# A hybrid encoder step on one Trainium2 core: running maximum in attention, scaling on ScalarE, side work moved from GpSimd to VectorE

## The reference, cut to what matters

```
h = x + 0.5 * post1(SwiGLU_1(pre1(x)))          # F1
u = pre_mix(h); z = u @ w_in                     # IP: q|k|v, rwkv r,k,v,lora, gates
A = differential attention(z)                    # 4 heads, two softmax maps each
B = RWKV-7 time mixing(z)                        # 8 heads of 64
h = h + post_mix((sigmoid(gA)*(A@w_o_att) + sigmoid(gB)*(B@w_o_rwkv)) @ w_out)   # OP
y = h + 0.5 * post2(SwiGLU_2(pre2(h)))           # F2

attention of one head:  a = softmax(s0) - lam * softmax(s1);  o = a @ v
                        o = o * rsqrt(mean(o*o) + EPS) * subln_g * (1 - lam_init)
token mix of RWKV:      zs = z + (prev - z) * mu         # r, k, v and the lora columns
output of RWKV:         out = (norm(y) * lnx_g + lnx_b + bonus) * g
```

## Time and profile before

| | |
|---|---|
| median of 3 runs | 3108.46 us (3101.37 to 3112.38) |
| the profiled execution's own time | 3106.88 us |
| its span, first to last instruction | 3105.1 us |
| PE busy | 3005.9 us (97%) |
| DVE busy | 1768.8 us (57%) |
| ACT busy | 1301.8 us (42%) |
| POOL busy | 593.9 us (19%) |
| mean granted TensorE clock | 0.988 |

### The profile page before, as it was taken

How to read it: one execution, slowest core, us unless ns; L and a number is a source line. 1 busy time by engine, 2 the same in 40 slices (tenths; PEclk the granted TensorE clock), 3 DMA queues, 4 the chain that set the end, 5 groups by cost and what they waited for, 6 DMA issues and landing times.

```text
span 3105.1 us, 59030 instructions
## 1 busy us (share of the span) xinstructions
PE 3005.9 (97%) x23912; PEld 2663.9 (86%) x23912; DVE 1768.8 (57%) x3001; ACT 1301.8 (42%) x2682; POOL 593.9 (19%) x850
## 2 busy tenths in 40 slices
PE   8999999999999999999989999999999999999997
PEld 8999989888888878899778798888787889899997
DVE  5456543644674463665666545757756846656444
ACT  4434444432434443533444444444534434444432
POOL 1001002312621421501501302303213201010000
PEclk9999999999999999999999999999999999999999
DMA  6445557644654664643644644526455424665443
GB/s 170 126 129 174 155 175 221 205 151 133 215 189 151 217 194 142 212 125 96 227 154 148 211 148 131 169 76 222 141 166 162 129 89 138 207 207 169 127 127 120
DMA packets 504493, 500.51 MB, mean 161 GB/s; under 512 B 29096, under 2 KB 402112, under 8 KB 504208
## 3 DMA queue, kind: packets, MB, share of 16 engines
q1 hardware_dynamic: 475968, 406.36, 42.1%
q0 software_dynamic: 28256, 90.39, 9.3%
HBM read 443.16 MB, written 54.47 MB: 160 GB/s over the span
## 4 chain that ended last, share of the span: by engine, by line
PE 88%; DVE 6%; issue 2%; ACT 2%; POOL 1%; DMA 1%; SPq 0%; ACTq 0%; POOLq 0%; DVEq 0%
PE ps L279 42%; PE ps L289 29%; PE ps L1065 5%; DVE wlo L243 1%; PE ps L1846 1%; PE ps L1830 1%; PE ps L301 1%; PE ps L1764 1%; PE ps L1057 1%; PE ps L1775 1%; PE ps L1801 1%; PE ps L1840 1%; PE ps L1070 1%; PE ps L1197 1%; ACT whi L235 1%
## 5 line engine op out<-in xcount | busy, mean ns | idle before, releaser
L243 DVE TENSOR_TENSOR wlo<-raw,whi 128x512 fp32r<-128x512 f32 x1140 | 823.1, 724 | 830.0 <-ACT whi L235 827.3
L235 ACT ACTIVATE whi<-raw 128x512 fp32r<-128x512 f32 x1140 | 712.6, 628 | 629.0 <-PE ps L279 348.3
L279 PE MATMUL ps<-xnhi,whi 128*128 128x384 f32 x2688 | 929.6, 346 | 3.4 <-DVE xnlo L556 3.4
L279 PE MATMUL ps<-xnhi,wlo 128*128 128x384 f32 x2688 | 903.2, 336 | 0.0
L279 PE MATMUL ps<-xnlo,whi 128*128 128x384 f32 x2688 | 902.4, 336 | 0.0
L279 PEld LDWEIGHTS ps<-xnhi,whi 128*128 128x128 f32 x2688 | 507.7, 189 | 28.9 <-issue 14.5
L279 PEld LDWEIGHTS ps<-xnlo,whi 128*128 128x128 f32 x2688 | 508.0, 189 | 2.7 <-issue 2.2
L279 PEld LDWEIGHTS ps<-xnhi,wlo 128*128 128x128 f32 x2688 | 507.0, 189 | 0.0
L289 PE MATMUL ps<-whi,hidhi 128*128 128x512 f32 x936 | 383.5, 410 | 13.8 <-DVE xnlo L556 9.7
L289 PE MATMUL ps<-whi,hidlo 128*128 128x512 f32 x936 | 367.9, 393 | 0.0
L289 PE MATMUL ps<-wlo,hidhi 128*128 128x512 f32 x936 | 367.6, 393 | 0.0
(11 more groups left out here) (310 smaller groups left out, 3411.8 us busy)
## 6 DMA issues: line engine op xcount, KB each, us to landing
raw<-in_ffn_w_in_dram SPq DMA_DIRECT2D x528, 256.0 KB, 3.0
raw<-in_ffn_w_out_dram SPq DMA_DIRECT2D x264, 256.0 KB, 2.9
raw<-in_w_in_dram SPq DMA_DIRECT2D x252, 256.0 KB, 3.0
xt<-h_scratch SPq DMA_DIRECT2D x42, 512.0 KB, 5.9
att<-in_cache_att_k_dram POOLq DMA_DIRECT2D x64, 256.0 KB, 4.8
att<-in_cache_att_v_dram POOLq DMA_DIRECT2D x64, 256.0 KB, 3.1
rw<-zr_scratch POOLq DMA_DIRECT2D x51, 256.0 KB, 7.5
raw<-in_w_out_dram SPq DMA_DIRECT2D x48, 256.0 KB, 3.1
```

The source lines that it names most:

```text
L235: act.activation(B["whi"][:, slot], B["raw"][:, slot], ACT.Copy).then_inc(E["whi"], 1)
L243: dve.tensor_tensor(B["wlo"][:, slot], B["raw"][:, slot], B["whi"][:, slot].bitcast(F32), ALU.subtract).then_inc(E["wlo"], 1)
L279: ins = pe.matmul(ps[:, bank, 0:BT], B["w" + wt][:, n % RING, i * P:(i + 1) * P], x(xt, i), start=first and i == 0 and (wt, xt) == passes[ ...
```

## The change

Six edits, which the diff shows. (1) In attention with two chunks the second chunk's maximum is taken together with the first's (a running maximum), so only the first chunk has to be rescaled later: one ACT exponential of two columns, one ACT pass over map 0's first 512 columns (`att_sc`). The softmax's common factor 1/sum of map 0 is left out of the weights; it comes back in the norm after V (as ACT's `scale` in the square and one more small product on POOL). The pass L2040 and one small operation go; the chunks are turned last first. (2) From the second stage on, x is scaled on ACT instead of DVE, and a pre norm has 9 steps. (3) The last post norm multiplies the gain in ahead of the mean square, in halves, and makes scale and residual one pass. (4) The token mixes of the recurrence move from POOL to DVE, one to two steps later or earlier; POOL keeps the loads; its waits for them and for the slots of the mixes go to DVE with the work (lines that only move are left out of the diff). (5) So do the four output operations of `C3` and `C4`. (6) `timetable()` counts a slot as 0.6 in the first 17 slots of OP and in slots 2 to 7 of a stage that follows on a whole stage with a post norm, so fewer side steps fall there; `O` costs 1.5.

```
-POST_STEPS, PRE_STEPS, POST_LEAD = 15, 8, 6
+POST_STEPS, PRE_STEPS, POST_LEAD = 15, 9, 6
...
+            for tl in range(NT):
+                if k:
+                    act.wait_ge(E["rstd"], 3 * (posts + pres) + tl + 1)
+                    act.wait_ge(E["squared"], squares)
+                    act.activation(B["xt"][:, tl], B["xt"][:, tl], ACT.Identity, scale=sums[:, 4 + tl:5 + tl]).then_inc(E["x2d"], 1)
+                yield
-            for _ in range(PRE_STEPS - 5):
+            for _ in range(PRE_STEPS - 8):
...
-            for _ in range(4):
-                yield
-                dve.wait_ge(E["rstd"], 3 * (posts + pres) + tl + 1)
-                dve.tensor_scalar(B["xt"][:, tl], B["xt"][:, tl], rstd[:, tl:tl + 1], None, ALU.mult).then_inc(E["x2d"], 1)
+                if k == 0:
+                    dve.wait_ge(E["rstd"], 3 * (posts + pres) + tl + 1)
+                    dve.tensor_scalar(B["xt"][:, tl], B["xt"][:, tl], rstd[:, tl:tl + 1], None, ALU.mult).then_inc(E["x2d"], 1)
-            for _ in range(PRE_STEPS - 7):
+            for _ in range(PRE_STEPS - 3):
...
-        for _ in range(POST_LEAD + 2):
+        def gained(tl, hf):
+            y = B["yb"][:, tl, hf * 512:(hf + 1) * 512]
+            dve.wait_ge(E["gain_in"], 16 * (posts + 1))
+            dve.wait_ge(E["squared"], 6 * (posts + pres) + 3 * hf + tl + 1)
+            dve.tensor_tensor(y, y, B["gB"][:, hf * 512:(hf + 1) * 512], ALU.mult).then_inc(E["scaled"], 1)
+        for step in range(POST_LEAD + 2):
+            if last and step >= POST_LEAD - 1:
+                gained(step - POST_LEAD + 1, 0)
+        if last:
+            for tl in range(NT):
+                gained(tl, 1)
+            for tl in range(NT):
+                dve.wait_ge(E["rstd"], 3 * (posts + pres) + tl + 1)
+                dve.wait_ge(E["xin%d" % tl], 16 * (posts + pres + 1))
+                dve.wait_ge(E["scaled"], 3 * posts + 4 + tl)
+                dve.scalar_tensor_tensor(B["yb"][:, tl], B["yb"][:, tl], rstd[:, tl:tl + 1], B["xt"][:, tl], ALU.mult, ALU.add).then_inc(E["h_done"], 1)
-                if step < NT:
-                    scale(step)
-                    add(step)
+                pass
...
+        lora = slot(S_L)
+        dve.wait_ge(E["rw_ld_l"], 48 * (p + 1))
+        own.do(dve.tensor_tensor(lora[:, 256:512], lora[:, 256:512], lora[:, 0:256], ALU.subtract))
+        own.do(dve.tensor_tensor(lora[:, 256:512], lora[:, 256:512], slot(S_ML)[:, 0:256], ALU.mult))
+        dve.tensor_tensor(lora[:, 0:256], lora[:, 0:256], lora[:, 256:512], ALU.add).then_inc(E["rw_zl"], 1)
+        dve.wait_ge(E["rw_ld_r"], 48 * (p + 1))
+        own.do(dve.tensor_tensor(slot(S_RP), slot(S_RP), slot(S_R), ALU.subtract))
+        own.do(dve.tensor_tensor(slot(S_RP), slot(S_RP), slot(S_MU), ALU.mult))
+        dve.tensor_tensor(slot(S_R), slot(S_R), slot(S_RP), ALU.add).then_inc(E["rw_mix"], 1)
+        dve.wait_ge(E["rw_ld_k"], 48 * (p + 1))
+        own.do(dve.tensor_tensor(slot(S_KP), slot(S_KP), slot(S_K), ALU.subtract))
+        own.do(dve.tensor_tensor(slot(S_KP), slot(S_KP), slot(S_MK), ALU.mult))
+        dve.tensor_tensor(slot(S_K), slot(S_K), slot(S_KP), ALU.add).then_inc(E["rw_mix"], 1)
+        dve.wait_ge(E["rw_ld_v"], 32 * (p + 1))
+        dve.wait_ge(E["rw_ld_mv"], 16 * (p + 1))
+        own.do(dve.tensor_tensor(slot(S_VP), slot(S_VP), slot(S_V), ALU.subtract))
+        own.do(dve.tensor_tensor(slot(S_VP), slot(S_VP), slot(S_MU), ALU.mult))
+        dve.tensor_tensor(slot(S_V), slot(S_V), slot(S_VP), ALU.add).then_inc(E["rw_mix"], 1)
...
+        dve.wait_ge(E["rw_ln"], 32 * (p + 1))
+        dve.wait_ge(*done(E, "yn", p + 1))
+        own.do(dve.tensor_tensor(y, y, slot(Z_LG if kd else S_LG), ALU.mult))
+        own.do(dve.tensor_tensor(y, y, slot(Z_LB if kd else S_LB), ALU.add))
+        own.do(dve.tensor_tensor(y, y, slot(S_BON), ALU.add))
+        dve.wait_ge(*done(E, "gg", p + 1))
+        dve.tensor_tensor(y, y, slot(S_GG), ALU.mult).then_inc(E["rw_out"], 1)
...
-        mix(l2[:, S_L, 0:256], l2[:, S_L, 256:512], l2[:, S_ML, 0:256]).then_inc(E["rw_zl"], 1)
-        mix(slot(S_R), slot(S_RP), slot(S_MU)).then_inc(E["rw_mix"], 1)
-        mix(slot(S_K), slot(S_KP), slot(S_MK)).then_inc(E["rw_mix"], 1)
-        mix(slot(S_V), slot(S_VP), slot(S_MU)).then_inc(E["rw_mix"], 1)
+        yield "G"
-        yield "G"
...
-            act.activation(st[:, 8:12], st[:, 8:12], ACT.Exp).then_inc(E["att_f"], 1)
+            act.activation(st[:, 8:10], st[:, 8:10], ACT.Exp).then_inc(E["att_f"], 1)
+            act.wait_ge(E["att_f"], two_before(n) + 1)
+            act.wait_ge(E["att_ex"], 2 * chunks_before(n + 1))
+            act.activation(V["ex"][0][:, 0:512], V["ex"][0][:, 0:512], ACT.Identity, scale=st[:, 8:9]).then_inc(E["att_sc"], 1)
-        for c, (a, e) in enumerate(chunks_of(tile)):
-            act.wait_ge(E["att_t"], chunks_before(n) + c + 1)
-            act.activation(V["awT"][:, a // P:e // P], ps[:, AB[c], 0:e - a].rearrange("p (k q) -> p k q", q=P), ACT.Copy).then_inc(E["att_tev"], 1)
+        for i, c in enumerate(turned(nc)):
+            a, e = chunks_of(tile)[c]
+            act.wait_ge(E["att_t"], chunks_before(n) + i + 1)
+            act.activation(V["awT"][:, a // P:e // P], ps[:, AB[i], 0:e - a].rearrange("p (k q) -> p k q", q=P), ACT.Copy).then_inc(E["att_tev"], 1)
...
-        act.activation(V["oh"][:, tile - TILE0[blk]], ps[:, AB[0], 0:P], ACT.Square, accum_out=st[:, 20:21]).then_inc(E["att_sq"], 1)
+        act.activation(V["oh"][:, tile - TILE0[blk]], ps[:, AB[0], 0:P], ACT.Square, scale=st[:, 12:13], accum_out=st[:, 20:21]).then_inc(E["att_sq"], 1)
...
-            dve.tensor_scalar(nb, nb, SCALE, None, ALU.mult).then_inc(E["att_nb"], 1)
-            if c == 1:
+            if c == 0:
+                dve.tensor_scalar(nb, nb, SCALE, None, ALU.mult).then_inc(E["att_nb"], 1)
+            else:
+                dve.scalar_tensor_tensor(nb, nb, SCALE, st[:, 0:2], ALU.mult, ALU.min).then_inc(E["att_nb"], 1)
-                own.do(dve.tensor_tensor(st[:, 12:14], st[:, 0:2], st[:, 2:4], ALU.min))
-                pair = lambda x: x.rearrange("p (c m) -> p c m", c=2)
-                dve.tensor_tensor(pair(st[:, 8:12]), st[:, 12:14].unsqueeze(1).broadcast_to([P, 2, 2]), pair(st[:, 0:4]), ALU.subtract).then_inc(E["att_df"], 1)
+                dve.tensor_tensor(st[:, 8:10], nb, st[:, 0:2], ALU.subtract).then_inc(E["att_df"], 1)
-        if nc == 1:
-            own.do(dve.reciprocal(st[:, 12:14], st[:, 4:6]))
-            own.do(dve.tensor_tensor(st[:, 16:18], st[:, 12:14], lamv, ALU.mult))
-        else:
+        total = st[:, 4:6] if nc == 1 else st[:, 14:16]
+        if nc == 2:
-            own.do(dve.tensor_tensor(st[:, 4:8], st[:, 4:8], st[:, 8:12], ALU.mult))
-            own.do(dve.tensor_tensor(st[:, 12:14], st[:, 4:6], st[:, 6:8], ALU.add))
-            own.do(dve.reciprocal(st[:, 12:14], st[:, 12:14]))
-            own.do(dve.tensor_tensor(st[:, 12:14], st[:, 12:14], lamv, ALU.mult))
-            own.do(dve.tensor_tensor(pair(st[:, 16:20]), pair(st[:, 8:12]), st[:, 12:14].unsqueeze(1).broadcast_to([P, 2, 2]), ALU.mult))
-        for d, (a, e) in enumerate(chunks_of(tile)):
+            own.do(dve.tensor_tensor(st[:, 4:6], st[:, 4:6], st[:, 8:10], ALU.mult))
+            own.do(dve.tensor_tensor(total, st[:, 4:6], st[:, 6:8], ALU.add))
+        own.do(dve.reciprocal(st[:, 12:14], total))
+        own.do(dve.scalar_tensor_tensor(st[:, 16:17], total[:, 0:1], neg_lam, st[:, 13:14], ALU.mult, ALU.mult))
+        for c in turned(nc):
+            a, e = chunks_of(tile)[c]
-            own.do(dve.tensor_scalar(x0, x0, st[:, 16 + 2 * d:17 + 2 * d], None, ALU.mult))
-            dve.scalar_tensor_tensor(x0, x1, st[:, 17 + 2 * d:18 + 2 * d], x0, ALU.mult, ALU.add).then_inc(E["att_aw"], 1)
+            ratio = st[:, 16:17]
+            if nc == 2 and c == 0:
+                ratio = st[:, 17:18]
+                own.do(dve.tensor_tensor(ratio, st[:, 16:17], st[:, 9:10], ALU.mult))
+                dve.wait_ge(E["att_sc"], two_before(n) + 1)
+            dve.scalar_tensor_tensor(x0, x1, ratio, x0, ALU.mult, ALU.add).then_inc(E["att_aw"], 1)
...
-        pool.tensor_tensor(st[:, 22:23], st[:, 22:23], halfc, ALU.pow).then_inc(E["att_rs"], 1)
+        pool.tensor_tensor(st[:, 22:23], st[:, 22:23], halfc, ALU.pow).then_inc(E["att_pw"], 1)
+        pool.wait_ge(E["att_pw"], n + 1)
+        pool.tensor_tensor(st[:, 22:23], st[:, 22:23], st[:, 12:13], ALU.mult).then_inc(E["att_rs"], 1)
...
+RW_COST = {"O": 1.5, "LD": 3, "ML": 2, "L": 1.5, "WA": 1.5, "G": 1.5, "CX": 1.5, "PD": 1.5, "P1": 1.5, "P2": 1.5, "P3": 1.5, "P4": 1.5, "C2": 1.5, "C3": 1.5, "C4": 1.5}
...
+    room = [1.0] * start[-1]
+    for k, (kind, blk) in enumerate(STAGES):
+        if kind == "OP":
+            for s in range(start[k], start[k] + 17):
+                room[s] = 0.6
+        if k and kind != "IP" and STAGES[k - 1][0] != "IP" and not spilled(k - 1):
```

(42 more changed lines are left out.)

## The result

The changed kernel takes 3114.58 us (median of 19 runs, 3110.53 to 3120.31), the kernel before 3107.24 (19 runs beside them): ratio 1.0024, 95% interval 1.0017 to 1.0031. I had forecast 3079, inside 3045 to 3118; 0.70 of the chance was on faster. The move is +7 us where −29 was forecast. The profiled span is 3112.4 us, the granted clock 0.988 as before.

A forecast was written before the change was run, and what follows sets the result against it. PE's waits and clock pace were taken as the bound. Net waits −19.5, clock −9 and tail −1 summed to −29.5 us, giving 3079 us, with a range for 8 in 10 of 3045 to 3118.

The forecast's parts named there:

- What bounds the kernel: Whole kernel: only PE's waits and pace count; about 75 us can be touched, 50 of waits and 25 of clock.
- DVE's queue: DVE's busy time: +91 us of moved work, −58 removed, −40 relief from POOL; about unchanged at 1760 us.
- The rest of the gain has to come from `room`: Attention's weight waits: fewer side steps at norms cut 2 us of backlog; waits 19.2 to 8 us (−11), bounds 0 and −19.
- the other waits are fixed in this change: PE's remaining waits: 5.5 us for the second head's load and 9.7 us of `xnlo` behind last turns stay.
- My rival for slower (C): DVE stands at the recurrence's load wait in eight tiles, 5.9 us each, +47 against −34: 3121 us; chance 0.15.
- Entries: Stage entries: PE's waits for `xnlo` and `tmp` go from 14.3 to 7 us (−7), bounds +5 and −12.
- POOL's mixes: Recurrence token mixes: PE's 2.5 us wait for POOL's first mix goes, with 1 us of the same kind: −3.5.
- The new wait: DVE's `LD` step: waits of 4 to 5.6 us for POOL's loads in three tiles cost PE 5 us; bounds 0 and 30.
- Attention: Attention with two chunks: first and last turns some 0.7 us earlier, 3.5 us over five waits; the rest from `room`.
- Tail: After the last matmul: three of six full-width passes remain, −1 us; bounds −2.5 and 0.
- Rival B: Nothing moves: DVE's total stays, mixes replace held time, L2041 waits stay near 15 us; 3104 us, chance 0.17.

The follow-up runs named there:

- e2: The kernel before with only the new slots of the side steps; ratio 1.0080, median 3130.0 us.
- e4: The kernel before with only the recurrence's token mixes and output operations moved from POOL to DVE; ratio 0.9995, median 3103.9 us.
- e9: The kernel before with only the attention edit, the running maximum, side steps in their old slots; ratio 0.9972, median 3098.7 us.
- e10: The kernel before with x scaled on ACT, pre norms of 9 steps and the new last post norm, old slots; ratio 0.9988, median 3103.7 us.
- e3: The changed kernel with the recurrence's token mixes and output operations back on POOL; ratio 1.0057 to the kernel before, median 3124.2 us.
- e6: e1 with DVE's lora mix one step later and the first head of blocks 2 and 3 loaded one POOL step earlier; ratio 0.9928 to the kernel before.
- e1: The changed kernel with the side steps in the slots of the kernel before; ratio 0.9974 to the kernel before, median 3097.4 us.
- e8: The kernel before with every step of the recurrence one slot later, attention where it was; ratio 1.0058, median 3123.6 us.
- e12: e6 with every step of the recurrence one slot earlier; median 3086.4 us, ratio 0.9931 to the kernel before.

## Why the prediction was wrong

- *What bounds the kernel*: right. PE's waits and its pace decide. Over the 13 kernels idle time runs from 83 to 115 us, PE's busy time from 2999.7 to 3015.1 roughly along with it. From before to e2 idle grew by 15.7, busy by 9.2: 0.6 of pace for each microsecond of wait, and a line through all 14 kernels gives 0.5. I took half. Single kernels leave the line: e4, e9 and e10 are 3.6 to 3.9 us less busy than the kernel before at nearly its idle time.
- *DVE's queue*: right in sign, mis-sized. +91 − 58 and −44.5 in all give 77.5 us of relief, not 40. The mixes alone show it more cleanly: +91 and DVE only 1.7 us busier (e4), so 89; from e3 to the changed kernel 18.9 busier, so 72. It moved PE little in the old slots (e4 is even) and by 10 us in the new (e3).
- **The step that failed**: "The rest of the gain has to come from `room`", with two or three steps fewer taken as 2 us of backlog. I priced it by the waits that would go, −11 with bounds of 0 and −19, and gave it no price for what comes in other places, though 552 of the two chains' 681 steps moved, by up to nine slots. The waits at L1840 did go, further than forecast (to 0 from 15.9). The new ones cost more: +25 us alone, +16 beside the others. The upper bound of that edit should have been as large as the lower: it touches all 50 us of waits and can add as many. The same step made me write that "the other waits are fixed in this change": POOL's issues move with the slots, and the 5.5 us of the head load became 13.2. (That load is not the second head's but the first head's of the second block: e6 moves it and the wait goes.) My rival for slower (C) named another mechanism.
- *Entries*: L302 and `tmp` 9.3 us where I had 7. But the scale's leaving DVE did not do it: L301 has 13.4 in e10. Slots alone bring it to 8.4 (e2), all else without them to 8.2 (e1), both together to 3.6.
- *POOL's mixes*: right, the wait is gone.
- *The new wait*: right as a mechanism. In the new slots four waits of DVE, 16.3 us, longest 5.5 (forecast: three of 4 to 5.6), and PE stood 4.03 once. (1487.88 in the earlier trace rows is the issue of the third lora load, so the 9.2 us are counted from the last of them.) In the old slots five, 27.0, longest 11.0, with 12 us of PE waits behind them, over twice the term. C's price held there, its number of tiles did not.
- *Attention*: −8.7 alone, above the 3.5 of its chain plus clock. DVE is 26 us less busy in e9 (1742.8), and the turns' waits go from 16 to 9 us, 7 where the chain alone would give 3.5. That the rest comes from a shorter backlog is likely and not shown apart.
- *Tail*: right. It lasted 15.8 us after 16.5.
- *Rival B*: wrong for the change as a whole, since its L1840 waits "stay near 15" and they went. But its premise, that the mixes on DVE just take the place of the held time, is what e4 shows: 89 us of relief for 91 of mixes. DVE's queue became emptier by what edits (1) and (2) took away. The Trainium skill's sentence that moving work between GpSimd and DVE might not help ("Perfetto Trace Analysis", Optimizing Scalar/DVE Operations) agrees with e4, in DVE's busy time and in time (0.9995); in the new slots the same move was worth 10 us (e3).

The parts with old slots sum to −8.7 − 1.6 − 3.7 = −14.0 us; together (e1) they gave −8.1. That they partly remove the same waits would be the plain reading, but the profiled idle times do not bear it out: −1.2, −1.4 and +1.9 us alone, −5.7 together. So the cause of this gap stays open. Left open too is why the rule for `O` and due time costs 13 us: no run parts these two.

## What to carry to other kernels

When two side chains are woven by slot into a PE-bound stream, any edit that moves them is an edit of all waits: give it a range to both sides, time it apart from the edits that come with it, and keep the old slots while judging those. Then mend single waits by what stands ahead in the queue: move a DMA issue ahead of a step that waits, and a wait for a DMA behind the step that doesn't need it. The two mends here gave 12 to 14 us in the old slots and 15 to 16 in the new, more than the change's other five edits together (8).

## What the runs showed of the hardware

Taking 194 us of two-input operations from POOL shortened DVE's instructions by 72 us (e3 against the changed kernel) to 89 us (e4), about what the same operations cost on DVE (91). `wlo` ran at a mean of 689 ns (690 in e4, 721 in e3 with the mixes back on POOL), like the 692 that the earlier trace rows showed for a stretch without POOL. Two waits of PE of 4.4 and 4.7 us in a stretch with nearly none brought 7.7 us more of idle time and 7.6 us more of busy time at a lower granted clock (e2: 0.98 for 1.00). That a shift of one slot, 2.6 us, can cost 18 us (e8) or nothing (e12) is what I had least expected. ACT's 128x1024 scale from SBUF took 1140 ns where the pass from PSUM had 1027.
